# Forget-gate mixer of a four-part model: gate piece first, head norms by pairs, scores of two head pairs ahead of v's last unit, output projection begun on half of its input

## The chip, the cores and the metric

The kernel runs on one core of a Trainium2 chip. The metric is the time of one execution in device microseconds (us); the time before is the median of three runs.

## The reference

The model has 256 tokens of width 1024 and runs an even mixer, an expert layer, the forget-gate mixer (`fox_mix`), a second expert layer, a further mixer and a feed-forward layer. The change touches `fox_mix` alone (16 heads of 64):

```python
p = h @ w_in
q, k, v, fz = jnp.split(p, [hd, 2 * hd, 3 * hd], axis=-1)
q = rms_norm(q per head, q_g);  k = rms_norm(k per head, k_g)
c = jnp.cumsum(jax.nn.log_sigmoid(fz + fgate_b), axis=1)
logits = q @ k.T * scale + c[q position] - c[k position]   # causal, in two blocks of 128 queries
o = softmax(logits) @ v
return o @ w_out
```

## The kernel before

**Pieces.** Weights come in pieces of 128x1024 floats through a ring of three slots, loaded by SyncE's queue. ScalarE rounds a piece to a high part (`high(k)`, recorded at L508), and VectorE or GpSimd subtracts for the low part (`low(k)`, L1036 on VectorE, L404 on GpSimd); the table `RUNS` fixes which. TensorE makes three products for each piece: high by high, high by low, low by high (16 + 8 matmuls of 256 columns in `features` and `token_unit`). `high(k)` waits until piece k-3 is used up, and the load of piece k+3 waits for `low(k)`.

**The mixer's 25 input pieces.** Pieces 0 to 5 are made ahead of the input's norm. Before the change, pieces 6 to 15 are the rest of q and k (five units of two pieces), piece 16 is the gate fz, and 17 to 24 are v (four token units of two pieces). Low parts of 2 to 13 are VectorE's, those of 14 to 24 GpSimd's. After the gate piece ScalarE and VectorE make its log sigmoid (`log_sigmoid_rows`) and the running sum; ScalarE's queue stores 16 rows of it (L876) and, after the second v unit, spreads them to all 128 partitions (L879, 2 MB). GpSimd masks the spread table with two affine selects (L458) once it has made all low parts to piece 24.

**Head norms.** q and k lie in eight groups of 512 columns (0 to 3 q, 4 to 7 k). Squares (ACT, L872), sums over a head by TensorE (L2406, `head_sums`), logarithm and exponential (L573, L578, `roots`), and the product with the gain (VectorE, L1628) follow in order 0 to 7, three, three and two groups behind the first three v units.

**Attention.** `fox()` on three engines handles a pair of heads per step. TensorE: `scores` (8 matmuls, L2357), two `turn` (three transposes each, L2365), two `mix` (L2373 to L2375). VectorE: `mask` (L1584) adds the table and finds the maximum; it copies out the odd head's turned scores (L1590). ScalarE: `exps` (L833, L834) and the even head's copy (L839). Scores, turned scores and masks of head h share bank h % 4, so `scores(j)` waits for both copies of pair j-2. Before the change the order on TensorE is `scores(j+1)`, `turn` of pair j, `mix` of pair j-1; on ScalarE it is

```python
for j in range(FH // 2):
    exps(2 * j)
    if j:
        turned_out(2 * j - 2)
    exps(2 * j + 1)
```

After the mixes VectorE scales with the inverse sums (`scale_half`, L1599), TensorE turns the result (`back`, L2383), ScalarE and VectorE split it (L845, L1606), and `add_to_stream` projects it with eight pieces of w_out (25 to 32 of the mixer). VectorE adds these to the stream (L1124).

## Time and profile before

| | us |
|---|---|
| median of 3 runs | 2280.3 (2279.82 to 2280.7) |
| profiled execution, its time | 2284.43 |
| profiled execution, its span | 2281.5 |
| TensorE busy in the span | 2234.4 (98%) |
| forget-gate mixer, from its first matmul to the end of the last sum into the stream | 958.1 to 1102.1 |

The span runs from the first to the last instruction; its profile gives for each engine when an instruction started, how long it took, and what its engine had waited for. The granted clock of TensorE is given as a share of 2.4 GHz. Matmul ends are modelled and overlap their successors, so the distance from start to start is what a matmul costs.

### The profile page before, as it was taken

How to read it: one execution, taken by the hardware profiler on the slowest of the kernel's cores; microseconds unless marked ns; L12 is line 12 of the kernel's file. 1: busy time of each engine (PE TensorE's matmuls, PEld its weight loads, DVE VectorE, ACT ScalarE, POOL GpSimd, SP SyncE). 2: the span in 40 equal slices, each digit the busy share in tenths (PEclk: the TensorE clock that was granted, in tenths of full speed). 3: DMA queues.
4: the chain of work that ended last, by engine and by line, in shares of the span. 5: the costliest groups of instructions: out<-in, count | busy, mean ns of one | idle time of the engine just before them, and what ended most of it. 6: DMA issues, size and time to landing. Idle time of an engine off the chain costs nothing.

```text
span 2281.5 us, 43893 instructions
## 1 busy us (share of the span) xinstructions
PE 2234.4 (98%) x14296; PEld 1939.1 (85%) x14296; DVE 1568.1 (69%) x3187; ACT 1189.8 (52%) x1888; POOL 774.2 (34%) x766
## 2 busy tenths in 40 slices
PE   8999999999999999998999999999999999999999
PEld 7889888888888888897988888888888888888877
DVE  6733885888888755545258768888886555535885
ACT  4145555555444455565455565554444556556764
POOL 0027888222332000033778862223320002664000
PEclk9999999999999999998999999999999999999999
DMA  5345655555555566552555655555556655444655
GB/s 159 102 128 157 188 190 175 178 173 170 172 174 173 177 193 194 181 183 88 163 157 188 186 183 167 173 165 176 174 175 185 193 193 176 135 135 152 189 175 165
DMA packets 109649, 385.62 MB, mean 169 GB/s; under 512 B 12512, under 2 KB 14848, under 8 KB 109312
## 3 DMA queue, kind: packets, MB, share of 16 engines
q1 hardware_dynamic: 106864, 382.34, 53.7%
q10 hardware_dynamic: 2704, 2.23, 0.3%
q8 instruction: 47, 0.77, 0.1%
q14 instruction: 34, 0.28, 0.0%
HBM read 383.46 MB, written 1.06 MB: 169 GB/s over the span
## 4 chain that ended last, share of the span: by engine, by line
PE 93%; DVE 3%; ACT 1%; DMA 1%; issue 1%; POOL 1%; SPq 0%; DVEq 0%; ACTq 0%; POOLq 0%
PE bank L1998 23%; PE bank L1978 12%; PE bank L2048 11%; PE bank L2050 11%; PE bank L2049 11%; PE bank L1895 3%; PE bank L1907 3%; PE bank L1899 3%; PE bank L2104 3%; PE bank L2287 3%; PE bank L2230 1%; PE bank L2255 1%; PE bank L2098 1%; PE bank L2153 1%; DVE x_parts L1077 1%
## 5 line engine op out<-in xcount | busy, mean ns | idle before, releaser
L508 ACT ACTIVATE w_hi<-ring 128x1024 fp32r<-128x1024 f32 x689 | 727.8, 1057 | 544.6 <-PE bank L2050 403.4
L404 POOL TENSOR_TENSOR w_lo<-ring,w_hi 128x1024 fp32r<-128x1024 f32 x226 | 544.4, 2415 | 800.1 <-ACT w_hi L508 784.7
L1036 DVE TENSOR_TENSOR w_lo<-ring,w_hi 128x1024 fp32r<-128x1024 f32 x463 | 567.9, 1227 | 235.2 <-ACT w_hi L508 229.6
L1998 PE MATMUL bank<-x_parts,w_hi 128*128 128x512 f32 x2320 | 586.2, 394 | 0.2 <-ACT w_hi L508 0.2
L1998 PEld LDWEIGHTS bank<-x_parts,w_hi 128*128 128x128 f32 x2320 | 416.6, 189 | 74.8 <-issue 0.4
L2048 PE MATMUL bank<-w_hi,x_parts 128*128 128x512 f32 x1112 | 439.3, 395 | 0.9 <-DVE x_parts L1043 0.9
L2050 PE MATMUL bank<-w_lo,x_parts 128*128 128x512 f32 x1112 | 433.6, 390 | 0.0
L2049 PE MATMUL bank<-w_hi,x_parts 128*128 128x512 f32 x1112 | 432.5, 389 | 0.0
L1978 PEld LDWEIGHTS bank<-x_parts,w_lo 128*128 128x128 f32 x2368 | 324.8, 190 | 25.0 <-DVE w_lo L1036 2.9
L416 POOL COPY quads<-sco 128x32 f16 (+1 forms) x256 | 169.8, 691 | 514.2 <-DVE sco L1494 514.1
L1978 PE MATMUL bank<-x_parts,w_lo 128*128 128x256 f32 x2368 | 336.7, 282 | 0.2 <-DVE w_lo L1036 0.2
L2050 PEld LDWEIGHTS bank<-w_lo,x_parts 128*128 128x128 f32 x1112 | 208.7, 188 | 44.5
L2048 PEld LDWEIGHTS bank<-w_hi,x_parts 128*128 128x128 f32 x1112 | 208.9, 188 | 43.2 <-DVE w_lo L1036 0.9
L2049 PEld LDWEIGHTS bank<-w_hi,x_parts 128*128 128x128 f32 x1112 | 209.1, 188 | 41.9
L1895 PE MATMUL bank<-x_parts,w_hi 128*128 128x256 f32 x720 | 181.3, 289 | 9.3 <-ACT x_parts L533 7.9
L1899 PE MATMUL bank<-x_parts,w_hi 128*128 128x256 f32 x656 | 160.8, 283 | 0.0
L1895 PEld LDWEIGHTS bank<-x_parts,w_hi 128*128 128x128 f32 x720 | 138.6, 192 | 15.4 <-issue 8.8
L734 ACT ACTIVATE sco<-bank 128x256 f32<-128x256 f32 x136 | 52.2, 384 | 183.8 <-PE bank L1978 183.8
L1486 DVE TENSOR_TENSOR sco<-iota,quads 128x512 f16<-128x512 f16 (+1 forms) x256 | 130.3, 551 | 7.1 <-POOL quads L416 7.1
L1899 PEld LDWEIGHTS bank<-x_parts,w_hi 128*128 128x128 f32 x656 | 125.8, 192 | 0.1
L1043 DVE TENSOR_TENSOR x_parts<-big,x_parts 128x256 fp32r<-128x256 f32 x278 | 116.2, 418 | 0.0
L734 ACT ACTIVATE big<-bank 128x256 f32<-128x256 f32 x120 | 45.9, 384 | 130.9 <-PE bank L1978 130.8
(299 smaller groups left out, 2511.9 us busy)
## 6 DMA issues: line engine op xcount, KB each, us to landing
ring<-u_dram SPq DMA_DIRECT2D x256, 512.0 KB, 3.5
ring<-v_dram SPq DMA_DIRECT2D x256, 512.0 KB, 3.5
ring<-up_dram SPq DMA_DIRECT2D x44, 512.0 KB, 3.6
ring<-wq_dram SPq DMA_DIRECT2D x32, 512.0 KB, 3.6
ring<-sb_in_dram SPq DMA_DIRECT2D x31, 512.0 KB, 3.6
ring<-od_in_dram SPq DMA_DIRECT2D x25, 512.0 KB, 3.6
ring<-down_dram SPq DMA_DIRECT2D x22, 512.0 KB, 3.6
ring<-ev_in_dram SPq DMA_DIRECT2D x21, 512.0 KB, 3.6
```

Of the source, the lines that this page charges most:

```text
L404: pool.tensor_tensor(w_lo[:, k % RING, :], ring[:, k % RING, :], w_hi[:, k % RING, :].bitcast(F32), ALU.subtract).then_inc(g["lo_pool"], 1)
L416: last = pool.tensor_copy(dst[:, at + r], v.to_broadcast([P, GROUP_T, QUAD]))
L508: A(w_hi[:, k % RING, :], ring[:, k % RING, :], ACT.Copy).then_inc(g["w_hi_done"], 1)
L1036: V.tensor_tensor(w_lo[:, k % RING, :], ring[:, k % RING, :], w_hi[:, k % RING, :].bitcast(F32), ALU.subtract).then_inc(g["lo_dve"], 1)
L1486: return V.tensor_tensor(fours(dst), keys.to_broadcast(shape), of_token[:, row].to_broadcast(shape), ALU.is_equal)
L1895: mm(dst, hi[:, rows[c]], xh[:, c, :], start=(c == 0), stop=False)
L1899: mm(dst, hi[:, rows[c]], xl[:, c, :], start=False, stop=False)
L1978: return mm(dst[:, 0:T], lo[:, rows[c]], xh[:, c, :], start=False, stop=False, skip_group_check=True)
L1998: mm(dst[:, :], hi[:, rows[c]], x_both[:, c, :], start=(c == 0), stop=False, skip_group_check=True)
L2048: mm(dst, xh[:, s, t], hi[:, cols], start=False, stop=False, skip_group_check=True)
L2049: mm(dst, xl[:, s, t], hi[:, cols], start=False, stop=False, skip_group_check=True)
L2050: last = mm(dst, xh[:, s, t], lo[:, cols], start=False, stop=False, skip_group_check=True)
```

## The change

- Order of pieces: the gate is piece 6, the rest of q and k are 7 to 16, and v stays at 17 to 24. VectorE makes low parts to 16, GpSimd 17 to 24. `log_sigmoid_rows` follows piece 6; on VectorE it stands between `low` of piece 9 and `low` of piece 10. The rows are stored after q and k's unit 4 and spread after unit 5.
- GpSimd waits for the spread table and masks it ahead of the low part of piece 17.
- Head norms go in the order q0, k0, q1, k1, ..., so that `scores(0)` and `scores(1)` need only two of them. The last two groups are normed inside `fox()`.
- TensorE issues `scores(0)` and `scores(1)`, then v's last unit into bank 4, then per step `turn` of pair j, `mix` of pair j-1, `scores(j+2)`. ScalarE does `exps` of four heads first, then copies v out, then per step one copy and two `exps`; it rounds pieces 26 and 27 in steps 2 and 3.
- `back(0)` stands in step 6. The projection of output pieces 0 to 2 (25 to 27 of the mixer) is done in two halves of the input: the first halves of all three ahead of `back(1)`, one of them ahead of the last two mixes. The scaling is cut in eight instead of four.

```diff
@@ -55,7 +55,9 @@
-SUM_GROUPS = [(0, 1, 2), (3, 4, 5), (6, 7), ()]
+SUM_ORDER = (0, 4, 1, 5, 2, 6, 3, 7)
+SUM_GROUPS = [(0, 1, 2), (3, 4, 5), (6, 7)]
+OD_ORDER = tuple(range(6)) + (16,) + tuple(range(6, 16)) + tuple(range(17, 25))
@@ -253,8 +255,8 @@
-                ("od_in", "od_in", 2, POOL), ("od_in_b", "od_in", 12, DVE),
-                ("od_in_c", "od_in", 11, POOL), ("od_out", "od_out", 8, POOL),
+                ("od_in", "od_in", 2, POOL), ("od_in_b", "od_in", 15, DVE),
+                ("od_in_c", "od_in", 8, POOL), ("od_out", "od_out", 8, POOL),
@@ -317,6 +319,8 @@
+                    if array == "od_in":
+                        return a[array][OD_ORDER[j]]
@@ -451,7 +455,6 @@
-                    lows("od_in_c", 0, 11)
@@ -459,6 +462,7 @@
+                    lows("od_in_c", 0, 8)
@@ -844,43 +848,59 @@
+                roots([(o_n[:, s * 512:(s + 1) * 512], bank[6 + k][:, :]) for k, s in enumerate(SUM_ORDER[6:])], HD,
+                      "od_log", "od_root", 6, "od_sum")
+                for h in range(4):
+                    exps(h)
+                n[0] += 2
+                A(token_major(o_v, D, 3), b3(bank[4][:, :], TB), ACT.Copy).then_inc(g["units_out"], 1)
+                u[0] += 1
                 for j in range(FH // 2):
-                    exps(2 * j)
-                    if j:
-                        turned_out(2 * j - 2)
-                    exps(2 * j + 1)
-                turned_out(FH - 2)
-                high_half(0)
+                    turned_out(2 * j)
+                    if j + 2 < FH // 2:
+                        exps(2 * j + 4)
+                        exps(2 * j + 5)
+                    if 1 <= j <= RING:
+                        highs(n[0] + j)
+                    if j == 6:
+                        high_half(0)
...
-            unit_loop(5, lambda i, q: o_qk[:, bass.ds(i * 1536 + (3 * 512 + q * 512), 512)])
+            def o_unit(s):
+                unit(o_qk[:, s * 512:(s + 1) * 512])
+            o_unit(3)
...
+            o_unit(4)
+            act.wait_ge(g["od_bias_ready"], 1)
+            act.dma_start(rows_dram, o_z[5][0:FH, :]).then_inc(g["fox_rows_out"], 16)
+            o_unit(5)
+            act.wait_ge(g["fox_rows_out"], 16)
+            act.dma_start(fx_tab.rearrange("p (h t) -> p h t", h=FH)[:, :, P:3 * P],
+                          rows_dram.partition_broadcast(P)).then_inc(g["fox_rows_spread"], 16)
+            o_unit(6)
+            o_unit(7)
-            for j in range(4):
-                for s in SUM_GROUPS[j]:
-                    A(o_sq[:, s * 512:(s + 1) * 512], o_qk[:, s * 512:(s + 1) * 512], ACT.Square).then_inc(g["od_sq"], 1)
+            for j in range(3):
+                for k in SUM_GROUPS[j]:
+                    v = slice(SUM_ORDER[k] * 512, (SUM_ORDER[k] + 1) * 512)
+                    A(o_sq[:, v], o_qk[:, v], ACT.Square).then_inc(g["od_sq"], 1)
-                if j == 0:
-                    act.wait_ge(g["od_bias_ready"], 1)
-                    act.dma_start(rows_dram, o_z[5][0:FH, :]).then_inc(g["fox_rows_out"], 16)
-                if j == 1:
-                    act.wait_ge(g["fox_rows_out"], 16)
-                    act.dma_start(fx_tab.rearrange("p (h t) -> p h t", h=FH)[:, :, P:3 * P],
-                                  rows_dram.partition_broadcast(P)).then_inc(g["fox_rows_spread"], 16)
-                roots([(o_n[:, s * 512:(s + 1) * 512], bank[4 + s % 4][:, :]) for s in SUM_GROUPS[j]], HD,
-                      "od_log", "od_root", 3 * j, "od_sum")
-            highs(n[0] + 3)
+                if j < 2:
+                    roots([(o_n[:, SUM_ORDER[k] * 512:(SUM_ORDER[k] + 1) * 512], bank[4 + k % 4][:, :]) for k in SUM_GROUPS[j]], HD,
+                          "od_log", "od_root", 3 * j, "od_sum")
@@ -1561,7 +1581,7 @@
-                dve.wait_ge(g["units_out"], u[0] + 9)
+                dve.wait_ge(g["units_out"], u[0] + 4)
@@ -1594,10 +1614,11 @@
-                    for b in range(TB):
-                        of_head = inv[:, 8 * b:8 * b + 8].rearrange("p (h o) -> p h o", o=1).to_broadcast([P, 8, HD])
-                        V.tensor_tensor(b3(fx_y[:, b * D + half * 512:b * D + half * 512 + 512], 8),
-                                        b3(bank[4 + 2 * half + b][:, :], 8), of_head, ALU.mult).then_inc(g["fox_scaled"], 1)
+                    for q in range(2):
+                        for b in range(TB):
+                            of_head = inv[:, 8 * b + 4 * q:8 * b + 4 * q + 4].rearrange("p (h o) -> p h o", o=1).to_broadcast([P, 4, HD])
+                            V.tensor_tensor(b3(fx_y[:, b * D + half * 512 + q * T:b * D + half * 512 + (q + 1) * T], 4),
+                                            b3(bank[4 + 2 * half + b][:, q * T:(q + 1) * T], 4), of_head, ALU.mult).then_inc(g["fox_scaled"], 1)
@@ -1607,24 +1628,26 @@
+                for h in range(4):
+                    mask(h)
                 for j in range(FH // 2):
-                    mask(2 * j)
-                    if j:
-                        turned_out(2 * j - 1)
-                    mask(2 * j + 1)
+                    turned_out(2 * j + 1)
+                    if j + 2 < FH // 2:
+                        mask(2 * j + 4)
+                        mask(2 * j + 5)
-                turned_out(FH - 1)
+                    if j == 6:
+                        low_half(0)
-                low_half(0)
-            def head_norm(first, count, raw, dst, gain, root, ready):
-                for s in range(first, count):
+            def head_norm(order, raw, dst, gain, root, ready):
+                for k, s in enumerate(order):
-                    dve.wait_ge(g[root], s + 1)
+                    dve.wait_ge(g[root], k + 1)
@@ -1662,11 +1685,13 @@
-            for k in range(5, 12):
+            for k in range(5, 8):
+            for k in range(8, 15):
+                low(starts["od_in_b"] + k)
-            head_norm(0, 8, o_qk, o_n, of_qk, "od_root", "od_qk_ready")
+            head_norm(SUM_ORDER, o_qk, o_n, of_qk, "od_root", "od_qk_ready")
@@ -1919,15 +1944,17 @@
-            def token_unit():
+            def token_unit(to=None):
...
+                if to is None:
+                    to = unit_bank(u[0])
...
-                        dst, t = unit_bank(u[0])[:, b * T:(b + 1) * T], slice(b * P, (b + 1) * P)
+                        dst, t = to[:, b * T:(b + 1) * T], slice(b * P, (b + 1) * P)
                         for c in range(4):
@@ -1936,7 +1963,7 @@
-                        dst, t = unit_bank(u[0])[:, b * T:(b + 1) * T], slice(b * P, (b + 1) * P)
+                        dst, t = to[:, b * T:(b + 1) * T], slice(b * P, (b + 1) * P)
                         for c in range(4):
@@ -2347,7 +2374,7 @@
                 def scores(j):
-                    pe.wait_ge(g["od_qk_ready"], 4 + j // 2 + 1)
+                    pe.wait_ge(g["od_qk_ready"], 2 * (j // 2) + 2)
@@ -2375,8 +2402,8 @@
                 def back(half):
-                    pe.wait_ge(g["fox_scaled"], 2 * half + 2)
+                        pe.wait_ge(g["fox_scaled"], 4 + 2 * (j + 1) if half else 4)
@@ -2384,26 +2411,63 @@
+                both_low = 4 * xs[0] + 2
+                ready = next_split()
+                def projected(j, half, w, ready=None):
+                    hi, lo, low_ready = w
+                    low_ready()
+                    dst = bank[4 + j // 2][:, (j % 2) * T:(j % 2 + 1) * T]
+                    for c in range(4 * half, 4 * half + 4):
+                        if ready:
+                            ready[0](c)
+                        rows = slice(c * P, (c + 1) * P)
+                        mm(dst, hi[:, rows], xh[:, c, :], start=(c == 0 and j % 2 == 0), stop=False, skip_group_check=True)
+                        mm(dst, lo[:, rows], xh[:, c, :], start=False, stop=False, skip_group_check=True)
+                    for c in range(4 * half, 4 * half + 4):
+                        if ready:
+                            ready[1](c)
+                        last = mm(dst, hi[:, c * P:(c + 1) * P], xl[:, c, :], start=False, stop=False, skip_group_check=True)
+                    return last
+                pe.wait_ge(g["units_out"], u[0])
+                scores(1)
+                pe.wait_ge(g["od_log"], 5)
+                token_unit(bank[4])
                 for j in range(FH // 2):
-                    if j + 1 < FH // 2:
-                        scores(j + 1)
+                    if j == 1:
+                        pe.wait_ge(g["units_out"], u[0])
...
-                back(0)
+                    if j + 2 < FH // 2:
+                        scores(j + 2)
+                    if j == 6:
+                        back(0)
+                w = [weights_in_turn(j, 0) for j in range(RING)]
+                pe.wait_ge(g["x_lo_done"], both_low)
+                projected(0, 0, w[0])
+                projected(1, 0, w[1])
+                projected(2, 0, w[2])
-                pe.wait_ge(g["x_lo_done"], 4 * xs[0] + 2)
-            def head_sums(s, src, done, mean):
-                if s >= 4:
-                    pe.wait_ge(g[mean], s - 3)
+                for j in range(RING):
+                    projected(j, 1, w[j], None if j else ready).then_inc(g["pieces_used"], 1)
+                n[0] += RING
+                for j in range(RING, 8):
+                    features(bank[4 + j // 2][:, (j % 2) * T:(j % 2 + 1) * T], weights_in_turn(0, 0)).then_inc(g["pieces_used"], 1)
+                    n[0] += 1
+            def head_sums(k, s, src, done, mean):
+                if k >= 4:
+                    pe.wait_ge(g[mean], k - 3)
-                    last = mm(bank[4 + s % 4][rows, :], one[rows, :].to_broadcast([64, 64]), src[rows, s * 512:(s + 1) * 512],
+                    last = mm(bank[4 + k % 4][rows, :], one[rows, :].to_broadcast([64, 64]), src[rows, s * 512:(s + 1) * 512],
@@ -2411,17 +2475,14 @@
-            one_unit(features, ready=next_split())
-            unit_loop(4)
-            one_unit(features, 1)
-            for j in range(4):
+            one_unit(features, 1, ready=next_split())
+            unit_loop(5)
+            for j in range(3):
-                for s in SUM_GROUPS[j]:
-                    pe.wait_ge(g["od_sq"], s + 1)
-                    head_sums(s, o_sq, "od_sum", "od_log")
-            pe.wait_ge(g["units_out"], u[0])
+                for k in SUM_GROUPS[j]:
+                    pe.wait_ge(g["od_sq"], k + 1)
+                    head_sums(k, SUM_ORDER[k], o_sq, "od_sum", "od_log")
-            add_to_stream()
```

## Rows read from the trace of the kernel before

**Rows 1.** The page: busy time by engine, and the low parts on VectorE.

```profile
PE 2234.4 (98%) x14296; PEld 1939.1 (85%) x14296; DVE 1568.1 (69%) x3187; ACT 1189.8 (52%) x1888; POOL 774.2 (34%) x766
...
L1036 DVE TENSOR_TENSOR w_lo<-ring,w_hi 128x1024 fp32r<-128x1024 f32 x463 | 567.9, 1227 | 235.2 <-ACT w_hi L508 229.6
```

**Rows 2.** Windows: length, busy PE, PEld, DVE, ACT, POOL (instructions), clock, DMA share, GB/s.

```profile
1040.05:1081.05 41.00, 34.95 (x251) 30.35 (x249) 19.41 (x82) 22.06 (x78) 6.95 (x3) 0.83 0.12 39
...
1045.30:1055.50 10.20, 9.51 (x46) 8.12 (x47) 4.33 (x22) 5.28 (x21) 1.70 (x1) 0.50 0.32 107
1072.00:1076.00 4.00, 2.33 (x22) 2.20 (x21) 1.92 (x4) 1.09 (x2) 0.00 (x0) 0.99 0.00 0
...
1963.20:1967.30 4.10, 0.00 (x0) 0.00 (x0) 4.10 (x4) 0.60 (x1) 2.25 (x1) 0.94 0.52 146
1967.30:1970.10 2.80, 2.72 (x26) 2.72 (x28) 0.03 (x1) 0.00 (x0) 0.00 (x0) 0.50 0.39 158
```

**Rows 3.** Timeline, TensorE: end of q and k, norm sums, first scores.

```profile
1008.22 1.12 PE L1907 MATMUL bank<-x_parts,w_lo 128*128 128x256 f32 x8
...
1032.37 1.93 PE L2406 MATMUL bank<-big,one 64*64 64x512 f32 x8
...
1040.93 0.93 PE L2357 MATMUL bank<-big 64*128 64x128 f32 x8 [0.69 <-ACT big L588]
```

**Rows 4.** Timeline, gate chain on VectorE, first and last of its five instructions.

```profile
1009.80 0.87 DVE L1566 TENSOR_SCALAR big<-big 128x256 f32<-128x256 f32 x1 [15.31 <-ACT big L588]
...
1012.97 0.69 DVE L1575 TENSOR_TENSOR_SCAN big<-big 128x256 f32<-128x256 f32 x1
```

**Rows 5.** Timeline, the issue of the spread, and the DMA view of its flight.

```profile
1023.81 0.41 ACTq L879 DMA_DIRECT2D big<-rows_dram  x1
...
q10 hardware_dynamic: 2064, 2.10, 56.8%
q1 hardware_dynamic: 377, 1.37, 31.8%
...
big<-rows_dram ACTq DMA_DIRECT2D x1, 2048.0 KB, 11.0
```

**Rows 6.** Timeline, GpSimd masks and low parts, and a group of norms on VectorE.

```profile
1034.98 4.42 POOL L458 TENSOR_SCALAR_AFFINE_SELECT big<-big 128x2048 f32<-128x2048 f32 x2 [0.82 <-DMA big<-rows_dram]
...
1040.03 2.35 POOL L404 TENSOR_TENSOR w_lo<-ring,w_hi 128x1024 fp32r<-128x1024 f32 x1 [0.47 <-DVE big L1628]
...
1028.72 5.98 DVE L1628 SCALAR_TENSOR_TENSOR big<-big,qk_gain 128x512 f32<-128x512 f32 x3 [4.83 <-ACT big L578]
```

**Rows 7.** Timeline, ScalarE: logarithm, high part and two exponentials of the last norms.

```profile
1033.49 0.69 ACT L573 ACTIVATE big<-bank,eps_row 128x512 f32<-128x512 f32 x1 [0.42 <-PE bank L2406]
...
1034.93 1.05 ACT L508 ACTIVATE w_hi<-ring 128x1024 fp32r<-128x1024 f32 x1
1035.88 1.14 ACT L578 ACTIVATE big<-big 128x512 f32<-128x512 f32 x2
```

**Rows 8.** Timeline, one step of the attention at full clock, on TensorE and ScalarE.

```profile
1059.39 0.93 PE L2357 MATMUL bank<-big 64*128 64x128 f32 x8
...
1062.45 0.38 PE L2357 MATMUL bank<-big 64*128 64x128 f32 x2
...
1060.99 0.40 ACT L833 ACTIVATE big<-big 128x128 f32<-128x128 f32 x1 [0.80 <-DVE big L1584]
...
1061.89 0.47 ACT L839 ACTIVATE big<-bank 128x384 f32<-128x384 f32 x1
```

**Rows 9.** Timeline, a copy on ScalarE and the scores that waited for it.

```profile
1045.43 0.47 ACT L839 ACTIVATE big<-bank 128x384 f32<-128x384 f32 x1
...
1045.99 1.62 PE L2357 MATMUL bank<-big 64*128 64x128 f32 x7 [0.75 <-ACT big L839]
```

**Rows 10.** Timeline, the last turn back, and the last sum into the stream.

```profile
1075.68 1.56 PE L2383 MATMUL bank<-ident,big 128*128 128x128 f32 x7 [1.67 <-DVE big L1599]
...
1101.41 0.69 DVE L1124 TENSOR_TENSOR xT<-bank,xT 128x512 f32<-128x512 f32 x1 [5.06 <-PE bank L1907]
```

6 lines of the change are left out of this document (3 added, 3 removed).

## The prediction

> **What bounds the kernel now.** I read the page first: TensorE is busy 98% of the span [rows 1], so only its waits and its slow stretches can be won. The windows by stage then place them: from the end of v's last unit (1040.05) to the end of the first projection piece (1081.05) TensorE has 34.95 us of busy time in 41.00, at a mean granted clock of 0.83 [rows 2]. Inside lies a stretch of 10.2 us at 0.50, that is at 1.2 GHz. The timelines give the chain. All four v units and the eight norm sums run without a gap; then the first scores wait 0.69 us for v's copy [rows 3], and the attention starts cold. Later a step takes 1062.45 - 1059.39 = 3.06 us, and TensorE fills it [rows 8]. At the end a turn back waits 1.67 us for the scaling, and the last sum into the stream starts at 1101.41 [rows 10].
>
> From the end of the norm sums (1032.37 + 1.93 = 1034.30, [rows 3]) to 1101.41 is 67.1 us. The work in it at full clock: an input or output piece has 24 matmuls at 0.12 us, 2.88 us (8 of its matmuls are the row at 1008.22 with 1.12 modelled, 0.96 to the next start [rows 3]). v's last unit is 5.76, the projection 23.04, eight pair steps 8 x 3.0 = 24.0 ([rows 8], rounded), two turns back 1.8: together 54.6. So 12.5 us are waits and half clock. That is all the change can win here, 0.55% of the span.
>
> **Part 1, the gate first.** Nothing is added to TensorE: piece 6 takes the role of the first split piece, and q and k end at 1009.2 as before. On VectorE the five gate instructions take 1009.80 to 1013.66, 3.9 us with the waits for ScalarE between them [rows 4]. They now stand in front of the low part of piece 10, which takes 1.23 us [rows 1]: 5.1 us after the end of piece 8, while TensorE wants that low part 2.88 + 1.92 = 4.8 us after it. Queued behind are the low parts of 11 to 16 and through them ring loads, which have some 3 us of room. I take 0.5 us of wait, bounds 0 and 1.0.
>
> **Part 2, GpSimd's order.** This is the term that decides. The spread is issued with the copy of unit 5, after 13 pieces: 1009.2 - 4 x 2.88 = 997.7, and 0.2 more to the copy and 0.5 of part 1: 998.4. Its flight took 11.0 us, with 2.10 MB of its own beside 1.37 MB of ring [rows 5]. The new place has ring loads at 2.88 us a piece beside it, so again two to three. Landing: 1009.4. GpSimd starts masks 0.1 later, needs 4.42 us, and 0.2 for the rest: 1014.1. Only then comes the low part of piece 17, 2.4 us by the row from 1040.03 [rows 6]: 1016.6. TensorE wants it when the high matmuls of piece 17 are through: 1009.2 + 0.5 + 1.92 = 1011.6. **Wait 5.0 us**. Before, the same masks stood behind the low parts, beside work. Piece 18 onward has its low part in time (2.4 each against 2.88 a piece). Bounds: if the flight scaled with its own bytes alone, 11.0 x 2.10 / 3.47 = 6.7 us, wait 0.7; with three full ring loads, 11.0 x 3.67 / 3.47 = 11.6, wait 5.6. I take the measured flight, since its neighbours are the same. By the Trainium skill (DMA: Bandwidth & Descriptors, "Where 436 GB/s comes from") 16 ports allow about 435 GB/s, which would put 2.10 MB at 4.8 us, and with the fixed cost of about 2 us that the page gives under its latency facts the wait would be under 1 us; the trace disagrees (11.0 us for the flight), with the ring's loads beside it.
>
> **Part 3, the clock behind that wait.** At 1963.20 TensorE stood 4.1 us, its clock fell to 0.50 before it resumed, and 2.8 us of work ran at half [rows 2]; half of that is 1.4 us lost. The same stall length stands in part 2. I take 1.4, bounds 0 and 3.
>
> **Part 4, scores ahead.** Norms 6 and 7 now lie on the path: they come after the last sums, behind their logarithms (0.69), a high part (1.05) and their exponentials (1.14 for two) [rows 7]. A norm took 5.98 / 3 = 2.0 us beside GpSimd's low parts [rows 6]; VectorE issues all eight ahead of its first mask. From the end of the sums: logarithm and high part to 1.7, exponentials to 2.8, norms to 5.7, first mask 6.3, four `exps` at 0.90 each ([rows 8], 1061.89 - 1060.99) to 9.9, v's copy 0.6, first copy of turned scores 0.5: 11.0. TensorE has scores 1.7, v unit 5.8, two turns 1.1: 8.6. So `scores(2)` waits 2.4 us. The v unit hides what the first step cost before; bounds 1 and 4.
>
> **Part 5, the step.** Here the new order costs. On ScalarE the copy of pair j now stands behind two `exps` that need `scores(j+1)`; before, behind one. Scores end to first `exps` is 1060.99 - 1060.32 = 0.67 (1060.32 is where 1059.39 + 0.93 ends), two `exps` 1.80, copy start to next scores 1045.99 - 1045.43 = 0.56 [rows 8, 9], scores 0.9: 3.9 us a step, against 3.06. That is 0.85 of wait in each of five steps, 4.3. Two high parts (1.05 each, [rows 7]) stand in the same queue in steps 2 and 3 and lengthen them: 2.0. `back(0)` waits for the masks of pair 7 and the scaling in four parts: 1.0. Waits of the loop: 7.3, bounds 3 (if work of a step is longer than I count) and 9.
>
> **Part 6, the tail.** `back(1)` waited 1.67 us before and the turns ran slow [rows 10]. Now 2 x 1.44 us of first halves lie there; the split of the last two quarters on ScalarE and VectorE still leaves 0.9 us. So parts 4 to 6 leave 2.4 + 7.3 + 0.9 + 0.3 (`turn(1)`) = 10.9 us of waits where there were 12.5 of waits and slow clock: **-1.6 us**, if the clock stays up.
>
> **Part 7, does it stay up?** From 1072 to 1076 TensorE stood some 1.7 us, and the clock fell at the end of it to 0.5 (the row's mean is 0.99) [rows 2]; its next matmuls, from 1075.68, ran slow [rows 10]. The new loop has gaps of 2.4 us and twice about 1.9 us, of the same size. A fall like that at 1045.3, 10.2 us long [rows 2], makes two steps of 5.5 us instead of 3.9: +3.2. One gap may well miss it. I take +1.6, bounds 0 and 6. The Trainium skill (TensorE: Matmul & The Clock Gate, "HAM oscillation") describes falls in DMA waits of 3 to 5 us. The gaps here are shorter, so by it this term would be 0 and the forecast 1.6 us lower; the row from 1072 speaks against it, since TensorE stood less than 2 us in it.
>
> **Sum.** 0.5 + 5.0 + 1.4 - 1.6 + 1.6 = +6.9 us. The profiled execution took 2284.43 with a span of 2281.5; it would become about 2291.3, and the median 2280.3 becomes **2287.2 us**.
>
> **Rivals.**
> - *The table is no hold, not slower.* If the spread lands within 11.0 - 5.0 = 6.0 us of its issue, parts 2 and 3 vanish: 2280.3 + 0.5 - 1.6 + 1.6 = 2280.8. For it: alone it might be there in 6.7. Against it: ring loads never stop there. From here a clock that stays up gives 2279.2.
> - *The clock stays up in the loop.* Part 7 is 0, and part 3 at its low bound: 2280.3 + 0.5 + 5.0 - 1.6 = 2284.2. For it: in steps with only 0.85 us of gap it should hold.
> - *The step stays bound by TensorE, the other side.* If the masks of one pair and the `exps` run early enough for steps of 3.06, parts 5 and 7 lose 4.3 + 1.6 us: 2281.3; with a short flight of the spread too, 2275, faster. It decides where ScalarE's copy comes less than 2.2 us after the scores. Against it: ScalarE takes its instructions in their order, and both `exps` need those scores.
>
> **How the numbers follow.** A measurement of this kernel tells 0.2% (4.6 us) from no change. The forecast, 0.55; clock up, 0.20; no hold, 0.15; step bound by TensorE, 0.10. Slower by over 0.2% (above 2284.9) holds most of the first and a third of the second: 0.58. Faster (under 2275.7) has only the corner of the last two: 0.08. Within: 0.34. Range: the low end is the corner of no hold with the clock up, 2279; the high end takes the upper bounds of the wait (5.6), the slow clock (3) and half of part 7's (3): 2280.3 + 0.5 + 5.6 + 3 - 1.6 + 3 = 2290.8, so 2291. The forecast's own range is 2284.9 to 2291.
>
> **What would show it.** GpSimd's masks (affine selects) ahead of the low part of piece 17, starting near 1009.5, and a wait of TensorE of about 5 us before the low matmuls of piece 17, put down to GpSimd; a granted clock of 0.5 right after it. A short wait at piece 10. Scores and their successors at 3.9 us, with copies on ScalarE as releasers. A gap-free start of the projection's first halves and about 0.9 us before the second. I am wrong if the spread lands by 1004.5, or if the step is near 3.1 us.

## The result

| | before | changed |
|---|---|---|
| median | 2282.66 us (2279.82 to 2286.3, 6 runs) | 2293.05 us (2290.51 to 2297.21, 6 runs) |
| ratio of the times | | 1.0052, 95% interval 1.0042 to 1.0062 |
| profiled execution, its time | 2284.43 us | 2297.21 us |
| profiled execution, its span | 2281.5 us | 2295.5 us |

The change makes the kernel slower by 0.52% of 2282.66 us, 11.9 us (9.6 to 14.2). The forecast was +6.9 us and 2287.2 us, with a range up to 2291; the measured median lies above that range. Of the 5.9 us between 2293.05 and 2287.2, 2.4 are the base: it was 2280.3 us over three runs and is 2282.66 over six. The direction and the two places were right, the size was not.

### The profile page after: what moved, and what is told of

It reads as the page before. It is cut to its first block, busy times and chain, and to the rows that moved or that the text cites. A ratio compares the mean times of both kernels' runs of the same rounds, so it can differ in the third digit from the quotient of the medians.

```text
span 2295.5 us, 43898 instructions
## 1 busy us (share of the span) xinstructions
PE 2238.6 (98%) x14296; PEld 1942.6 (85%) x14296; DVE 1569.0 (68%) x3194; ACT 1189.3 (52%) x1888; POOL 766.5 (33%) x763
## 4 chain that ended last, share of the span: by engine, by line
PE 91%; DVE 3%; DMA 2%; ACT 2%; issue 1%; POOL 1%; SPq 0%; DVEq 0%; ACTq 0%; POOLq 0%
PE bank L2025 23%; PE bank L2005 12%; PE bank L2075 11%; PE bank L2077 11%; PE bank L2076 11%; PE bank L2131 3%; PE bank L2314 3%; PE bank L1920 3%; PE bank L1932 3%; PE bank L1924 2%; PE bank L2257 1%; POOL w_lo L408 1%; PE bank L2282 1%; DMA big<-rows_dram 1%; PE bank L2125 1%
## 5 line engine op out<-in xcount | busy, mean ns | idle before, releaser
L408 POOL TENSOR_TENSOR w_lo<-ring,w_hi 128x1024 fp32r<-128x1024 f32 x223 | 536.3, 2412 | 765.6 <-ACT w_hi L512 746.8
L2025 PEld LDWEIGHTS bank<-x_parts,w_hi 128*128 128x128 f32 x2320 | 416.6, 189 | 74.8 <-issue 0.4
L1920 PE MATMUL bank<-x_parts,w_hi 128*128 128x256 f32 x696 | 174.4, 288 | 9.6 <-ACT x_parts L537 8.0
L1924 PE MATMUL bank<-x_parts,w_hi 128*128 128x256 f32 x640 | 156.9, 283 | 0.0
L1920 PEld LDWEIGHTS bank<-x_parts,w_hi 128*128 128x128 f32 x696 | 133.2, 191 | 15.7 <-issue 9.1
L1924 PEld LDWEIGHTS bank<-x_parts,w_hi 128*128 128x128 f32 x640 | 122.7, 192 | 0.1
```

The lines of the kernel that those rows point to most:

```text
L408: pool.tensor_tensor(w_lo[:, k % RING, :], ring[:, k % RING, :], w_hi[:, k % RING, :].bitcast(F32), ALU.subtract).then_inc(g["lo_pool"], 1)
L1920: mm(dst, hi[:, rows[c]], xh[:, c, :], start=(c == 0), stop=False)
L1924: mm(dst, hi[:, rows[c]], xl[:, c, :], start=False, stop=False)
L2025: mm(dst[:, :], hi[:, rows[c]], x_both[:, c, :], start=(c == 0), stop=False, skip_group_check=True)
```

## The profile after

The waits of TensorE from 1005 to 1100, changed kernel (total, times, longest):

```profile
PE bank L1969 <- POOL w_lo L408: 7.7, 1, 7.7
PE bank L2384 <- issue: 5.6, 4, 1.9
PE bank L2384 <- ACT big L843: 0.7, 1, 0.7
PE bank L2426 <- ACT x_parts L849: 0.3, 1, 0.3
PE bank L2410 <- DVE big L1620: 0.2, 1, 0.2
```

Together 14.5 us, one of them more than half: the low matmuls of piece 17 (L1969) wait for GpSimd's low part. The same view of the kernel before:

```profile
PE bank L2365 <- ACT big L834: 2.2, 3, 1.3
PE bank L2383 <- DVE big L1599: 1.7, 1, 1.7
PE bank L2357 <- ACT big L839: 0.7, 1, 0.7
PE bank L2357 <- ACT big L588: 0.7, 1, 0.7
PE bank L2357 <- issue: 0.6, 1, 0.6
```

These are 5.9 us and no long one. "issue" as a releaser, 5.6 us in four times, is a gap for which the trace shows no semaphore event. All four stand ahead of scores (L2384), and the timelines of TensorE and ScalarE show what they are. First the chain behind the long wait, timeline of the changed kernel:

```profile
1000.67 0.41 ACTq L891 DMA_DIRECT2D big<-rows_dram  x1
...
1015.27 3.96 POOL L461 TENSOR_SCALAR_AFFINE_SELECT big<-big 128x2048 f32<-128x2048 f32 x2 [56.99 <-DMA big<-rows_dram]
1019.30 0.10 POOL L464 MEMSET eps_row<- 128x1 f32 x1
1019.36 7.00 POOL L408 TENSOR_TENSOR w_lo<-ring,w_hi 128x1024 fp32r<-128x1024 f32 x3
...
1021.75 2.08 PE L1969 MATMUL bank<-w_lo,x_parts 128*128 128x256 f32 x8 [7.68 <-POOL w_lo L408]
```

Read it upwards: TensorE at 1021.75 waits for a low part begun at 1019.36, that stands behind the masks of 1015.27, and those had waited for the spread issued at 1000.67. This is the forecast chain (masks ahead of low part 17) with a longer flight: 14.4 us where [rows 5] had 11.0. The DMA view of the flight and its windows (columns as in [rows 2]):

```profile
q10 hardware_dynamic: 2064, 2.10, 38.2%
q1 hardware_dynamic: 586, 2.12, 34.3%
...
big<-rows_dram ACTq DMA_DIRECT2D x1, 2048.0 KB, 14.4
```

```profile
1000.70:1012.20 11.50, 11.50 (x98) 11.50 (x97) 3.68 (x3) 5.37 (x8) 0.00 (x0) 1.00 0.96 349
1012.20:1015.10 2.90, 1.87 (x16) 1.66 (x14) 0.00 (x0) 2.87 (x6) 0.00 (x0) 1.00 0.21 68
1016.80:1026.50 9.70, 4.75 (x22) 4.75 (x23) 0.00 (x0) 1.06 (x1) 9.50 (x6) 0.50 0.29 84
```

The ring moved 2.12 MB beside it, not 1.37 [rows 5]. The DMA engines were busy for 11.5 us at 349 GB/s; after that came 2.9 us in which they were busy for only a fifth. Divided by the busy share the rate is nearly the same in both, 349 / 0.96 = 364 and 68 / 0.21 = 324 GB/s. So in the slow end it was not the transfer that crawled; by this estimate only some three of the 16 engines still had work. The third window is the clock: 9.7 us at 0.50, of which 4.75 us were work.

The steps of the attention, TensorE, and ScalarE's queue in one of them:

```profile
1056.14 0.93 PE L2384 MATMUL bank<-big 64*128 64x128 f32 x8 [0.74 <-ACT big L843]
...
1060.08 0.93 PE L2384 MATMUL bank<-big 64*128 64x128 f32 x8 [0.93 <-issue]
...
1064.02 0.93 PE L2384 MATMUL bank<-big 64*128 64x128 f32 x8 [0.92 <-issue]
...
1068.91 0.93 PE L2384 MATMUL bank<-big 64*128 64x128 f32 x8 [1.87 <-issue]
...
1073.80 0.93 PE L2384 MATMUL bank<-big 64*128 64x128 f32 x8 [1.87 <-issue]
...
1074.65 1.53 PE L2392 MATMUL bank<-ident,big 128*128 128x128 f32 x6
```

```profile
1065.63 0.40 ACT L837 ACTIVATE big<-big 128x128 f32<-128x128 f32 x1 [1.71 <-DVE big L1604]
...
1067.40 1.04 ACT L512 ACTIVATE w_hi<-ring 128x1024 fp32r<-128x1024 f32 x1
1068.34 0.47 ACT L843 ACTIVATE big<-bank 128x384 f32<-128x384 f32 x1
```

The steps are 1060.08 - 1056.14 = 3.94 us and 3.94, then 4.89 and 4.89, where [rows 8] had 3.06. The scores of 1068.91 start 0.57 us after the copy of 1068.34 (0.56 in [rows 9]): it is the copy that "issue" stands for. The copy is behind two heads' exponentials, which are behind the masks of the scores one step earlier (1064.02), and in this step behind a high part of 1.04 us too. At 1074.65 six turns take 1.53 us instead of 0.87: the clock has fallen.

## The experiments

Three lengths are compared. The median; the mixer, from the logarithm of its own norm to the logarithm of the next norm on ScalarE; and TensorE's mean granted clock over 1005 to 1105, from which 2 x (1 - clock) x 100 is the time at half clock. Each ratio is to runs of the kernel before that were made beside the run in question (their medians are 2281.9 to 2282.7 us), so ratios compare better than medians where two rows are close. The first and last rows of the mixer, changed kernel and third profile of the kernel before:

```profile
969.59 0.46 ACT L577 ACTIVATE big<-bank,eps_row 128x256 f32<-128x256 f32 x1
...
1119.59 0.46 ACT L577 ACTIVATE big<-bank,eps_row 128x256 f32<-128x256 f32 x1
```

```profile
969.14 0.45 ACT L573 ACTIVATE big<-bank,eps_row 128x256 f32<-128x256 f32 x1
...
1107.14 0.46 ACT L573 ACTIVATE big<-bank,eps_row 128x256 f32<-128x256 f32 x1
```

| kernel | median us (runs) | ratio to before, 95% | profiled: time | mixer | clock |
|---|---|---|---|---|---|
| before | 2282.66 (6) | | 2284.43 | 142.0 | 0.93 |
| before, second profile | | | 2286.7 | 143.7 | 0.91 |
| before, third profile | | | 2284.26 | 138.0 | 0.98 |
| changed | 2293.05 (6) | 1.0052 [1.0042, 1.0062] | 2297.21 | 150.0 | 0.91 |
| changed, again | 2294.0 (4) | 1.0047 [1.0031, 1.0062] | 2294.91 | 148.6 | 0.95 |
| table late | 2284.0 (11) | 1.0003 [0.9994, 1.0012] | 2284.9 | 140.3 | 0.97 |
| exponentials split | 2286.2 (11) | 1.0017 [1.0008, 1.0026] | 2284.36 | 141.4 | 0.97 |
| both | 2277.22 (6) | 0.9971 [0.9959, 0.9984] | 2277.57 | 133.7 | 1.00 |
| both, again | 2275.62 (8) | 0.9974 [0.9963, 0.9984] | 2275.82 | 132.6 | 1.00 |
| rows by GpSimd's queue | 2287.61 (9) | 1.0022 [1.0013, 1.0032] | 2289.71 | 145.5 | 0.91 |
| stream as a loop | 2290.65 (5) | 1.0040 [1.0027, 1.0054] | 2290.92 | 146.8 | 0.93 |
| wait filled | 2292.03 (5) | 1.0042 [1.0029, 1.0056] | 2291.91 | 147.7 | 0.97 |
| both, tail late | 2278.16 (11) | 0.9982 [0.9973, 0.9991] | 2279.13 | 133.5 | 1.00 |
| both, third head early, loop | 2274.81 (8) | 0.9973 [0.9963, 0.9984] | 2273.44 | 132.0 | 1.00 |

**The kernel before, again (c_before, and c_before2 as the last run).**

> The kernel before, unchanged, for a second profile. The mixer (from its first matmul to the start of the last sum into the stream) took 143.3 us in the first profile and 151.5 us in that of the changed kernel; the parts of the program ahead of it and behind it were 2.5 and 3.3 us longer there, in code that did not change. If those 5.8 us belong to the change, this profile shows the first profile's times outside the mixer (958.1 ahead, 1180.1 behind); if they are spread between executions, it may lie anywhere between. The mixer's 143.3 should come again within 1 us.

> The kernel before once more. Its two profiled executions took 2284.4 and 2286.7 us, 2 to 4 us above its median of 2282, with TensorE's clock at half for 13.7 and 17.1 us between 1005 and 1105 and a mixer of 142.0 and 143.7 us, while its single runs lie between 2279.6 and 2286.3. Theory that part of the 11.9 us that the mixer's length does not show is this draw: an execution near the median or under it has a shorter slow stretch and a mixer of 139 to 141 us, and time minus mixer stays at 2142 to 2143 us. Rival, that the changed kernels lose some 2 to 4 us outside the mixer: in an execution near 2282 us the mixer is still 142 us or more, and the time outside it 2140 us.

Its two rows of windows, first and third profile, from 1005 to 1105:

```profile
1005.00:1105.00 100.00, 92.50 (x689) 81.39 (x687) 40.74 (x106) 61.02 (x138) 47.26 (x21) 0.93 0.38 122
```

```profile
1005.00:1105.00 100.00, 92.10 (x717) 81.12 (x716) 42.29 (x109) 63.75 (x141) 49.32 (x22) 0.98 0.40 127
```

The waits of the third profile are those of the first, to a tenth of a microsecond, and yet its mixer is 4.0 us shorter. What differs is how long the clock stays at half: 14 us in the first, 18 in the second (0.91), 4 in the third. So a mixer of before is a draw between 138 and 144 us. Time minus mixer is 2142.4, 2143.0 and 2146.3 us (mean 2143.9) in the three, 2147.2 and 2146.3 in the two of the changed kernel, and in the nine other profiles of the table between 2141.5 and 2145.7 with a mean of 2143.8. The rival of the last run (2 to 4 us lost outside the mixer in every changed kernel) falls with that mean for the variants; for the changed kernel itself, whose two profiles lie 2.9 us above it on average, it isn't excluded, though the third profile of before lies as high. The theory's sum did not come out either: this execution had the short mixer and took 2284.26 us nonetheless. Median minus 2143.9 gives the mixer of a median execution, if the mean of three holds: 138.8 before, 149 to 150 changed. By this estimate the first profile of before, on which the prediction was built, had a mixer some 3 us longer than a usual one.

**The changed kernel, again (c_after2).**

> The changed kernel once more, beside the three others of this group, to see what of its profile repeats. If the wait at piece 17 comes from the spread's place, the spread is in flight some 14 us again (13.8 to 15.0 in four profiles with this order, 10.7 and 11.0 in two of before), TensorE waits 7 to 8 us ahead of the low matmuls of piece 17 and its clock is at half for about 10 us around that. If the wait of the first profile was a chance of that execution, it lies near 5 us. Ratio to before 1.004 to 1.006.

Wait at piece 17: 7.69 us, flight 14.4, steps as above. The wait is a fixed part of this order. The half clock behind it lasted from 1020.4 to 1027.2 here, 6.8 us instead of about 10, of which 4.1 us were work (5.2 in the first profile, counted to the end of its slow stretch at 1026.9), and the half clock in the loop 3.4 us instead of 6.8. The first turn back waited 0.8 us instead of 0.2. Halved, the slow work makes 0.5 + 1.7 - 0.6 = 1.6 us, and the mixer is 1.4 us shorter.

**Table late (e1_table_late).** GpSimd makes four low parts ahead of its wait for the spread.

```
+                    lows("od_in_c", 0, 4)
                     pool.wait_ge(g["fox_rows_spread"], 16)
...
-                    lows("od_in_c", 0, 8)
+                    lows("od_in_c", 4, 8)
```

> The changed kernel with one edit: GpSimd masks the spread table behind the low part of piece 20 instead of ahead of that of piece 17. Theory (the wait for the table and the slow clock behind it are the loss): the 7.7 us wait of TensorE goes, and with it the 10 us at half clock that cost 2.6 us of work, so 10.3 us less than the changed kernel: about +1.6 us or 0.1% over before. Rival 1 (the loss moves): the masks now hold up the low part of piece 21, TensorE waits there 2 to 4 us, and the kernel stays 4 to 6 us slower than before. Rival 2 (the loss lies outside the mixer): no more than 5 us come back.

GpSimd's timeline and TensorE's waits from 1005 to 1100:

```profile
1012.29 9.50 POOL L408 TENSOR_TENSOR w_lo<-ring,w_hi 128x1024 fp32r<-128x1024 f32 x4 [54.70 <-ACT w_hi L513]
1021.75 3.95 POOL L462 TENSOR_SCALAR_AFFINE_SELECT big<-big 128x2048 f32<-128x2048 f32 x2
```

```profile
PE bank L2385 <- issue: 5.6, 4, 1.9
PE bank L2385 <- ACT big L844: 0.7, 1, 0.7
PE bank L2427 <- ACT x_parts L850: 0.3, 1, 0.3
PE bank L2411 <- DVE big L1621: 0.2, 1, 0.2
```

The wait at piece 17 is gone, all others stayed to a tenth, though the spread flew 14.5 us here too. The mixer is 149.3 (mean of two) - 140.3 = 9.0 us shorter, the median 2293.5 (mean of two) - 2284.0 = 9.5 us lower. That is the wait of 7.7 and the slow clock behind it. With this alone the change is even with before.

**Exponentials split (e2_exps_split).** ScalarE takes one head's exponentials ahead of the copy of turned scores and one behind it.

```
-                for h in range(4):
+                for h in range(2):
                     exps(h)
...
                 for j in range(FH // 2):
+                    if j + 1 < FH // 2:
+                        exps(2 * j + 2)
                     turned_out(2 * j)
-                    if j + 2 < FH // 2:
-                        exps(2 * j + 4)
-                        exps(2 * j + 5)
+                    if j + 1 < FH // 2:
+                        exps(2 * j + 3)
```

> The changed kernel with one edit: on ScalarE each step is one exps, the copy, the other exps, as before, with TensorE's new order kept. Theory (the copy that stands behind two exps sets the step): steps of 3.94 us fall to 3.1, the gaps of 0.93 and 1.87 us go or fall to the 1 us of a high part, and the clock doesn't fall at the loop's end; 5 to 7 us less than the changed kernel, so 0.2 to 0.3% over before instead of 0.5%. Rival (the step is set by TensorE's or VectorE's own work, the gaps only move): steps of 3.9 us stay and the time is that of the changed kernel within 1 us.

The four gaps of the steps are gone, with the high parts still in the queue; what is left are 7.1 us at piece 17, 1.3 at the third pair's scores, 0.8 at the first turn back, 0.3 at the second halves. The mixer is 149.3 - 141.4 = 7.9 us shorter and the median 7.3 lower. The waits fell by 5.0 us (14.5 to 9.5); the rest goes with the half clock, which no longer comes in the loop: the granted clock stays at 1.00 from 1024 to 1102.

**Both (e3_both, e3_again).**

> The changed kernel with both edits. Theory: the two losses are independent, so the gains add: 10.3 and 5 to 7 us less than the changed kernel, 4 to 6 us (0.2%) faster than before. Rival: without the long wait the attention starts at another phase of the other engines and the second edit gains under 2 us; then the time is that of the first edit alone.

> Both edits once more (table's masks behind the low parts of pieces 17 to 20, exponentials of a pair on either side of its copy), as the base of the two others of this group. Theory that the gain of 6.6 us was real: ratio 0.996 to 0.998, no wait at piece 17, steps of 3.07 us, no slow clock from 1005 to 1105, mixer of about 133.7 us. Rival, a lucky execution: a ratio of 0.998 to 1.000 and a mixer of 137 us or more.

TensorE's scores in the second profile:

```profile
1045.64 0.93 PE L2386 MATMUL bank<-big 64*128 64x128 f32 x8 [1.32 <-ACT big L844]
...
1048.70 0.93 PE L2386 MATMUL bank<-big 64*128 64x128 f32 x8
...
1051.77 0.93 PE L2386 MATMUL bank<-big 64*128 64x128 f32 x8
```

Steps of 3.06 us, no half clock from 1005 to 1105, and under before by 6.6 us in the medians, 5.9 us by the ratio (0.9974, interval 0.9963 to 0.9984: 3.7 to 8.4). The two edits together take off 2293.5 - 2276.4 = 17.1 us, singly 9.5 and 7.3: they add up. The rest of the change is thus worth more than it costs, once both holds are out.

**Rows by GpSimd's queue (e4_rows_gpsimd).** Both transfers of the gate's rows are issued by GpSimd as soon as the rows are ready.

```
+                    pool.wait_ge(g["od_bias_ready"], 1)
+                    pool.dma_start(rows_dram, o_z[5][0:FH, :]).then_inc(g["fox_rows_out"], 16)
+                    pool.wait_ge(g["fox_rows_out"], 16)
+                    pool.dma_start(fx_tab.rearrange("p (h t) -> p h t", h=FH)[:, :, P:3 * P],
+                                   rows_dram.partition_broadcast(P)).then_inc(g["fox_rows_spread"], 16)
                     pool.wait_ge(g["fox_rows_spread"], 16)
...
-            act.wait_ge(g["od_bias_ready"], 1)
-            act.dma_start(rows_dram, o_z[5][0:FH, :]).then_inc(g["fox_rows_out"], 16)
             o_unit(5)
-            act.wait_ge(g["fox_rows_out"], 16)
-            act.dma_start(...)
```

> The changed kernel with both transfers of the forget gate's rows (out to DRAM, and back spread over the partitions) issued from GpSimd's queue as soon as the rows are ready, near 992.5, and not from ScalarE's between its copies. In the changed kernel the first was issued at 994.9 and the spread at 1000.7. Theory that the wait at piece 17 is the spread's landing plus masks plus a low part, one for one: rows out 2.4 us earlier, the spread issued near 997.5; with the same flight (14.4 us) it lands near 1012 and not 1015, and the wait falls from 7.7 to about 4.5 us; time 3 to 4 us below the changed kernel. Rival, that the transfer ends when the ring's loads leave room and its issue matters little: it lands at 1015 again, wait 7 to 8 us, no change. A third outcome, that GpSimd's queue takes its descriptors slower, would give a longer flight and a wait of 8 us or more.

Its flight was 14.8 us. The spread's issue, the masks and the wait at piece 17, timeline:

```profile
994.53 1.20 POOL L461 DMA_DIRECT2D big<-rows_dram  x1 [1.48 <-DMA rows_dram<-big]
...
1009.52 3.97 POOL L466 TENSOR_SCALAR_AFFINE_SELECT big<-big 128x2048 f32<-128x2048 f32 x2 [13.79 <-DMA big<-rows_dram]
...
1016.01 2.08 PE L1969 MATMUL bank<-w_lo,x_parts 128*128 128x256 f32 x8 [2.64 <-POOL w_lo L408]
```

Counted from the mixer's first logarithm (968.87 here, 969.59 in the changed kernel), the masks start at 40.65 instead of 45.68, 5.0 us earlier, and the wait is 2.64 instead of 7.68, 5.0 us shorter: one for one. The median is 5.9 us under the mean of the two of the changed kernel, more than the 3 to 4 expected. The rows were out earlier than expected, since the first transfer took 1.8 us (5.2 in the changed kernel, from ScalarE's queue and 2.5 us later); no run tells the queue from the moment. The rival (it lands when the ring leaves room, at 1015 again) falls: it landed at 1009.3. But "the same flight" is luck in part: 3.06 MB of ring came in beside it, not 2.12, and it had no slow end. The last 2.9 us before it landed:

```profile
1006.50:1009.40 2.90, 2.90 (x27) 2.90 (x26) 1.22 (x1) 1.58 (x3) 0.00 (x0) 1.00 0.81 316
```

**Stream as a loop (e5_loop_kept).** The input pieces lie in memory in the new order, and SyncE's stream is a loop again.

```
-                    if array == "od_in":
-                        return a[array][OD_ORDER[j]]
...
-                loops = (count - done) // BODY if not array.startswith("ev_") and array != "od_in" else 0
+                loops = (count - done) // BODY if not array.startswith("ev_") else 0
```

> The changed kernel with the input pieces laid out in the new order in memory, so that SyncE's stream of them is a loop again as before, and not written out. Theory that the time lost outside the mixer (the changed kernel is some 11.9 us slower, its mixer only 7 to 8 us longer in the profile) comes from SyncE's longer program: 2 to 4 us below the changed kernel. Rival, that the rest is the difference between executions: the same time within 1.5 us. The wait at piece 17 stays near 7.7 us in both.

The windows of the flight (issued at 1000.44, in flight 12.9 us):

```profile
1000.50:1010.90 10.40, 10.40 (x89) 10.40 (x88) 3.67 (x3) 4.72 (x6) 0.00 (x0) 1.00 1.02 347
1010.90:1011.90 1.00, 1.00 (x11) 1.00 (x10) 0.00 (x0) 0.62 (x1) 0.00 (x0) 1.00 1.00 357
1011.90:1012.90 1.00, 1.00 (x11) 1.00 (x10) 0.00 (x0) 0.97 (x3) 0.00 (x0) 1.00 0.80 250
1012.90:1013.90 1.00, 0.93 (x8) 0.73 (x7) 0.00 (x0) 1.00 (x2) 0.40 (x1) 1.00 0.00 0
```

The ring's share is the same (2.11 MB), the rate too (347 GB/s), but the slow end is missing. The wait is 6.1 us instead of 7.7, the median 2.9 us under the mean of the two of the changed kernel, the mixer 2.5 us shorter. The intervals of the ratios overlap (1.0027 to 1.0054 here, 1.0031 to 1.0062 for "changed, again"), so the gain in time isn't clear of noise; what the trace shows is 1.6 us less of wait. Time minus mixer (2144.2 us) is that of the others, so the theory, which looked for the loss outside the mixer, finds no support. The other kernel with the loop (below) flew 12.9 us too; the eight with the written-out stream and the spread in ScalarE's queue flew 13.8 to 15.0. The edit changes two things, the loop and the place of the pieces in memory, and no run took them apart. Nor is a written-out stream enough for a slow end: "rows by GpSimd's queue" has it too and ended at 316 GB/s.

**The wait filled (e7_fill).** 56 extra matmuls between the high and the low matmuls of piece 17.

```
+                    if j == 0:
+                        for _ in range(fill):
+                            mm(bank[7][:, 0:T], xh[:, 0, t], hi[:, 0:T], start=True, stop=True)
                     low_ready()
```

> The changed kernel with 56 extra matmuls (128x128 on 128x256, into a bank that nobody reads before its next writer starts it anew) between the high and the low matmuls of piece 17, where TensorE waited 7.7 us. At 0.12 us each they fill 6.7 us of the wait. The masks, the low part and all that releases the wait are as they were. Theory that 2.5 us of the loss are the work run at half clock behind the wait (clock at half from 1016.8 to 1026.5): the clock stays up there and the time falls by about 2.5 us, with the low matmuls of piece 17 starting where they did. Rival, that the clock costs nothing on the path (the work behind it waits for something else anyway): no change within 1 us.

TensorE's timeline at piece 17:

```profile
1012.46 6.88 PE L1966 MATMUL bank<-w_hi,x_parts 128*128 128x256 f32 x56
1020.30 1.22 PE L1972 MATMUL bank<-w_lo,x_parts 128*128 128x256 f32 x8 [0.96 <-POOL w_lo L408]
```

The hold is the same (7.8 us from the first extra matmul to the low ones), but the eight low matmuls take 1.22 us and not 2.08: the clock stayed up. The median falls by 1.5 us (2293.5 - 2292.03), the mixer by 1.6 (149.3 - 147.7). The intervals of the two ratios overlap, so that the half clock costs time here is shown by the rows of the trace and only made likely by the medians. The 1.6 is less than the 2.4 us of the window above, and part of the gain is hidden: this profile's loop ran at half clock for 6.8 us, those of the changed kernel for 6.8 and 3.4.

**Both, with parts of the tail put back (e6_tail_late).** TensorE takes the last mixes and the second turn back ahead of all of the projection.

```
-                pe.wait_ge(g["x_lo_done"], both_low)
-                projected(0, 0, w[0])
                 mix(FH - 2)
                 mix(FH - 1)
+                back(1)
+                pe.wait_ge(g["x_lo_done"], both_low)
+                projected(0, 0, w[0])
                 projected(1, 0, w[1])
                 projected(2, 0, w[2])
-                back(1)
```

> Both edits, and of the changed kernel's own parts one undone: the first halves of the projection's three pieces are not interleaved with the last mixes, TensorE takes both last mixes and the second turn back first and the projection afterwards, as before the change. Theory that the interleaved first halves hide the scaling of the second half (0.83 us of wait behind them in the profile of both edits, 1.67 us at that place in the kernel before, and the parts of x after the turn): the second turn back waits 1.5 to 2 us again for the scaling, the second halves of the projection no longer wait, time 1.5 to 3 us above both edits. Rival, that the scaling in quarters alone was enough: within 0.5 us of it. If the gap makes the clock fall, 5 us or more.

The second turn back waits again, 1.14 us, less than the 1.67 of [rows 10] and less than expected; the wait of 0.3 at the second halves is gone. The mixer is 133.5 us against 133.7 and 132.6, the median 1.7 us above the mean of "both" (2276.4) and 2.5 above "both, again", which was run beside it. So the begun projection is worth something between 0 and 2.5 us; the intervals of the ratios overlap, and these runs tell no more.

**Both, the third head early (e8_third_exps).** The third head's exponentials stand ahead of v's copy, and SyncE's stream is a loop.

```
-                for h in range(2):
+                for h in range(3):
                     exps(h)
...
-                    if j + 1 < FH // 2:
+                    if 1 <= j < FH // 2 - 1:
                         exps(2 * j + 2)
```

> Both edits, with the third head's exponentials ahead of v's copy (ScalarE was idle there from 1042.7 to 1044.1) and not between it and the first copy of turned scores, and the input pieces laid out in the new order in memory, so that SyncE's stream is a loop. By the rows the copy at 1045.42 starts 0.87 us earlier and the wait of 1.33 us at the third pair's scores falls to about 0.5: 0.9 us below both edits. A theory that the written-out stream costs time elsewhere adds 1 to 3 us to that; its rival adds nothing.

The third pair's scores wait 0.74 us, now for VectorE's copy, instead of 1.32. The mixer is 132.0 us (132.6 in "both, again"), the median 0.8 under "both, again". It has the lowest median here, 7.4 us under before, but its ratio (0.9973, interval 0.9963 to 0.9984) can't be told from the 0.9974 of "both, again". The 0.6 us less of wait shows in the trace; a gain of 1 to 3 us more from the loop does not appear. The flight was 12.9 us here too, and with the table late nothing waits for it.

## Why the prediction was right in direction and short in size

The forecast was +6.9 us; the mean of the two ratios (1.00495) gives 0.00495 x 2282.5 = +11.3. Step by step:

- **Part 1**, 0.5 us for the gate in front: no wait at piece 10. The low part of piece 10 ran at 992.40, right behind the gate chain, was done at 993.6, and TensorE took it at 993.66. That was just in time: the chain took 6.6 us (985.91 to 992.48, 4.4 of them a wait for ScalarE) where 3.9 were counted, so its cost was too low and its room too small by about as much. Miss of 0.5, inside the bounds.
- **Part 2, the step that failed: the flight of the spread.** The chain was right link by link. From the start of the mixer the spread was issued where it was put (998.4 in the prediction's count; 1000.67 less the 2.5 us by which this execution's mixer began later, 998.2). The masks took 3.96 and not 4.42 us. But "the measured flight, since its neighbours are the same" was wrong: it took 14.4 us, not 11.0. The upper bound, 11.6, failed too. It scaled the flight by its bytes with three full ring loads; four came in (2.12 MB), which makes some 2 us: by the same rule 11.0 x 4.22 / 3.47 = 13.4, and the loop kernel, with the same bytes and no slow end, flew 12.9. The other 1.5 us are the slow end (2.9 us at 68 GB/s), for which the bound had no room. Wait 7.7 instead of 5.0: +2.7.
- **Part 3**, 1.4 us: the window gives 4.75 us of work at half clock, 2.4 us lost; the wait filled gives 1.5 (medians, not clear of noise). Up to +1.0.
- **Part 4**: `scores(2)` waited 0.74 us instead of 2.4. From the end of the sums (1047.3) the last norm was done after 3.7 us (1050.9) and not 5.7; the rest of the chain took what it was put at. The norm of 2.0 us [rows 6] was taken from a time when GpSimd worked beside it; here it idled:

```profile
1049.53 1.41 DVE L1651 SCALAR_TENSOR_TENSOR big<-big,qk_gain 128x512 f32<-128x512 f32 x2 [1.83 <-ACT big L582]
```

  That is 0.7 us each. And 2.0 is a mean of two kinds: in either kernel a norm takes about 0.74 us, or 2.4 to 2.9 when it meets a low part on GpSimd, as here, where it ends 0.5 us after the low part does:

```profile
1044.80 2.36 POOL L408 TENSOR_TENSOR w_lo<-ring,w_hi 128x1024 fp32r<-128x1024 f32 x1 [1.12 <-ACT w_hi L512]
1044.81 2.89 DVE L1651 SCALAR_TENSOR_TENSOR big<-big,qk_gain 128x512 f32<-128x512 f32 x1
```

  The Trainium skill (GPSIMD Engine Reference, "Specifications") says that GpSimd shares its port to SBUF with VectorE and that VectorE's instructions with two inputs from SBUF contend with it; a norm has two, and the trace agrees with 2.89 beside a low part and 0.7 without.
- **Part 5**: the step of 3.9 us came out at 3.94, with two high parts at 4.89. This is the best term of the forecast. But there were four gaps and not five: the fifth was filled, since the turns and mixes ahead of the last scores ran at half clock (1073.80 to 1078.57, 4.77 us without a gap). And the first turn back waited 0.2 us (0.8 in the second profile) and not 1.0: 5.8 us instead of 7.3.
- **Part 6**: 0.3 us of wait before the second halves, not 0.9.
- **Part 7**: the clock did fall once in the loop, right behind the second gap of 1.87 us, for some 6.8 us in the first profile and 3.4 in the second; in the profiles of "rows by GpSimd's queue" and "stream as a loop" it fell right behind the first of them. The Trainium skill (TensorE: Matmul & The Clock Gate, "HAM oscillation") describes falls in waits of 3 to 5 us; by these rows they come in rows of shorter gaps too.
- **Parts 4 to 6 as a sum**, "10.9 us of waits where there were 12.5", -1.6. The first number was too high by 4.1 us, since there were 6.8. The second belonged to an execution with an unusually long half clock: in the third profile of before the mixer is 4.0 us shorter with the same waits. Against a mixer of 138.0 these parts together win about 0.6 us (5.9 us of waits and, by that profile, some 1.5 us of slow work became 6.8 of waits) and lose some 2 in the loop's clock.

In the forecast's own terms the misses are -0.5 (part 1), +2.7 (2), +1.0 (3), +1.0 (4 to 6, -0.6 instead of -1.6) and +0.4 (7, 2 instead of 1.6), together 4.6 for 11.3 - 6.9 = 4.4. More than half is the flight.

Added up against that third profile: 7.7 + 2.4 + 6.8 - 5.9 + 2 - 1.5 = 11.5 us, for 149.3 - 138.0 = 11.3 us of mixer and 11.3 us of ratio. The 2 and 1.5 are estimates from rows at half clock (1.53 for 0.87 us at 1074.65, 1.53 for 1.04 at the turn back of the third profile).

Of the rivals, "the table is no hold" and "the step stays bound by TensorE" are what the two edits turn the kernel into: table late gives 2284.0 (the rival said 2280.8), both 2276.4 (it said 2275 with a short flight). Their mechanism was right, their condition wasn't met. "The clock stays up in the loop" did not occur. What stays open is why the flight ends with 2.9 us of little traffic (in the eight kernels with the written-out stream and ScalarE's queue in varying strength, in neither loop kernel, and not with GpSimd's queue), and how it would fare with fewer ring loads beside it: no run changed the ring's bytes alone.

## What to carry to other kernels

A transfer that an in-order engine waits for should stand behind all the work of that engine that doesn't need it: four low parts moved ahead of the wait were worth 9.5 us, with the flight as long as before. Where a copy releases the engine that is the bound, put at most one piece of work that depends on that engine's last output in front of it; splitting a pair of exponentials around the copy brought the step from 3.94 back to 3.06 us. And read a base from more than one profile where the clock falls in it: the same kernel with the same waits had 138, 142 and 144 us for one stage, and a change was costed against the 142.

## What the runs showed of the hardware

- A transfer of 2.10 MB that spreads 16 rows over all partitions took 10.3 to 11.0 us at one place and 12.9 to 15.0 us at another, beside ring loads of 512 KB; in four profiles with SyncE's stream written out it ended with 2.9 us at 40 to 88 GB/s, and not so in two where it was a loop over pieces in the order of memory, nor in one with the written-out stream and the spread in GpSimd's queue. The ring loads beside it took 7.2 to 8.0 us in the changed kernel's two profiles, and 3.4 to 3.6 where no spread was in flight. The flight's busy part had 349 GB/s in the changed kernel, and 387 over 7 us (1003.1 to 1010.1) in "exponentials split". By the Trainium skill (DMA: Bandwidth & Descriptors, "Where 436 GB/s comes from") the 16 ports carry some 435 GB/s and HBM's side for one core some 358; the 387 lies above the second and under the first.
- The same 16 KB out to DRAM took 1.8 us from GpSimd's queue and 4.0 to 5.3 us from ScalarE's at nearly the same place; in the kernel before it took 1.4 from ScalarE's, at another time.
- The clock stayed at half for 6.8 us around the end of one wait of 7.7 us and for about 10 around another, and for 4 to 18 us in 100 with the same waits in the kernel before. In the four profiles with both edits it never fell there.
